# Four half weight tiles ahead of the second half of the prompt, and turned parameter rows, at the start of a one-core decoder step

## The chip, the cores and the metric

The kernel runs on one core of a Trainium2 chip. A core has TensorE (PE: matrix products and transposes), VectorE (DVE), ScalarE (ACT), GpSimd (POOL) and SyncE (SP); SP and POOL issue most of the transfers between main memory and the core's memory. The metric is the device time of one execution in microseconds; the result is a median over executions.

## The reference, cut to what matters

One layer of a decoder trunk. The prompt (512 tokens) and eight samples are normalised, multiplied by one wide input matrix, and fed to three branches. All of it is in float32. The edit touches only the first steps: the normalisation, and the first product with the columns for q and k.

```python
def rmsnorm(x, g):
    xf = x.astype(jnp.float32)
    y = xf * lax.rsqrt(jnp.mean(xf * xf, axis=-1, keepdims=True) + EPS)
    return (y * g.astype(jnp.float32)).astype(x.dtype)
...
    h = rmsnorm(x, g_norm[l])
    a_u, a_v, a_z, b_q, b_k, b_v, b_gd, b_z, c_q, c_z, gl = split_proj(h, w_in[l])
...
    mk, mv = mem_kv(mem, g_mem[l], w_mem_kv[l])
```

`split_proj` is `h @ w_in` cut into pieces; D_MODEL is 1024. The memory tokens (256) are normalised with g_mem and multiplied with w_mem_kv.

## The kernel before, in words

The large products go through 17 blocks (NAMES: QK, K, V, BV, ...) of eight weight tiles. A weight tile is 1024 rows by 128 columns, held as eight 128x128 pieces. Each float32 product is made from three products of a high and a low part: ScalarE copies raw weights into w_hi (function `hi`, L512), VectorE subtracts to get w_lo (`lo`, L1156), and TensorE multiplies w_hi by h_lo, w_lo by h_hi and w_hi by h_hi. A tile takes 24 products over the first 256 tokens and 24 over the other 256 with the eight samples (264 columns). SP loads raw weights two tiles at a time into two buffers: tiles 0 and 1 from the first load, 2 and 3 from the second. Tile t is split two tiles ahead of its product; semaphore split_done counts the splits, prod_done the tiles done, evac_done those copied out of PSUM.

Every engine runs its own list in program order, and semaphores tie them together. There is no scheduler: the order in the code is the order on the engine.

The start is written by hand. The samples come first: ScalarE squares them (`square`, L517), VectorE scales them (L1490), TensorE turns them in eight transposes (L1084). Then for the first 256 tokens: ScalarE squares one block of 128 rows and VectorE the other (L1475), ScalarE takes the root (L536), VectorE the reciprocal (L1478), VectorE scales one block of rows (L1480) and ScalarE the other (L539), TensorE turns 16 pieces (L1094), ScalarE writes the high part with the gain g_norm (`x_hi_part`, L545) and VectorE the low part (`x_lo_part`, L1485). The transposes go through four banks of PSUM, so that each from the fifth on waits for a low part. TensorE then multiplies tiles 0 and 1 over these 256 tokens (L1101), turns the second 256 and multiplies the same two tiles over them; tiles 2 to 7 go as whole tiles through `project` (L865). Behind tile 3 stand the first transposes of the memory tokens (L888), whose squares ScalarE makes after it has copied out tile 1.

The gains are read by POOL as columns, one number to a partition: gn1, gm1, bg1, gnc, each with a transfer of its own:

```python
pool.dma_start(gn1[:, :], g_norm[0].rearrange("(k p) -> p k", p=P)).then_inc(sem("gn_loaded"), 16)
```

Of the kernel before, what the change touches and what calls it, by code (L numbers as in the profile page):

```python
# [68 lines left out]
X_A, X_B, X_M = 1, 1 + KT, 1 + 2 * KT  # L69
# [29 lines left out]
def bass_gated_parallel_step(nc, x_prompt, x_sample, state_gla, cache_mem_k, cache_mem_v,  # L99
# [19 lines left out]
    with ExitStack() as ctx:  # L119
# [47 lines left out]
        gn1 = sb("gn1", [P, KT])  # L167
        gm1 = sb("gm1", [P, KT])
        bg1 = sb("bg1", [P, 3 * KT])
        gnc = sb("gnc", [P, 2])  # L170
# [97 lines left out]

        def x_bank(u):

            return (p45, p67)[u // 2 % 2][:, u % 2, 0:HX]
# [50 lines left out]
        def _(pool):  # L322
# [22 lines left out]
            with nc.allow_non_contiguous_dma(reason="parameters by channel, a few KB"):  # L345
                pool.dma_start(gm1[:, :], g_mem[0].rearrange("(k p) -> p k", p=P)).then_inc(sem("gm_loaded"), 16)
                pool.dma_start(bg1[:, :], b_gate[0].rearrange("(k p) -> p k", p=P)).then_inc(sem("params_loaded"), 16)
                pool.dma_start(gnc[:, :], gn_g[0].rearrange("(k p) -> p k", p=P)).then_inc(sem("params_loaded"), 16)
                pool.dma_start(w00[:, :], w_s[0, :, 0, 0:1].rearrange("h o -> o h").broadcast_to([P, AH])).then_inc(sem("params_loaded"), 16)
                pool.dma_start(gd_raw[:, :, :], win[:, O_GD:O_GD + P].rearrange("(k p) c -> p k c", p=P)).then_inc(sem("params_loaded"), 16)  # L350
# [144 lines left out]
        def _(act):  # L495
# [24 lines left out]
            def mem_squares():  # L520
                act.wait_ge(sem("mem_loaded"), 16)
                link(square(mem_in[:, 0, :], junk, 5))
                act.wait_ge(sem("mem_sq"), 1)
                A(rstd[:, 5:5 + MT], ssq[:, 5:5 + MT], ACT.Sqrt, scale=1.0 / D, bias=eps_col[:, :]).then_inc(sem("rt_mem"), 1)

            def mem_hi_part(k):
                act.wait_ge(sem("gm_loaded"), 16)
# [3 lines left out]
            def x_roots(a):  # L531
# [6 lines left out]
                act.wait_ge(sem("x_rs"), a + 1)  # L538
                A(x0_in[:, 2 * a + 1, :], x0_in[:, 2 * a + 1, :], ACT.Copy,  # L539
                  scale=rstd[:, 2 * a + 1:2 * a + 2]).then_inc(sem("x_n_act"), 1)  # L540

            def x_hi_part(u):
                k, c0 = (u - X_A) % KT, HX * ((u - X_A) // KT)
                act.wait_ge(sem("xT_done"), u + 1)
                A(h_hi[:, k, c0:c0 + HX], x_bank(u), ACT.Copy, scale=gn1[:, k:k + 1]).then_inc(sem("xT_hi"), 1)  # L545

            act.wait_ge(sem("eps_ready"), 1)
            link(A(lstd, eps_col, ACT.Sqrt))
            act.wait_ge(sem("xs_loaded"), 16)
# [6 lines left out]
            for k in range(KT):  # L556
                x_hi_part(X_A + k)
                if k == 3:
                    hi(0, 0, 16)
# [1012 lines left out]
```

## Time and profile before

| what | value |
|---|---|
| median of 3 runs | 909.87 us (909.71 to 911.19) |
| the profiled execution's own time | 909.98 us |
| its span, first to last instruction | 908.2 us |
| PE busy | 870.3 us, 96% |
| DVE busy | 417.9 us, 46% |
| ACT busy | 395.7 us, 44% |
| POOL busy | 95.9 us, 11% |
| mean granted TensorE clock | 0.990 |

The busy time of an engine is the time in which it works at an instruction; waits and the issue of transfers are not in it. The two microseconds between the span and the execution's time lie around the program. The times in the trace count from the start of the span.

### The profile page before, as it was taken

How to read it: one execution, taken by the hardware profiler on the slowest of the kernel's cores; microseconds unless marked ns; L12 is line 12 of the kernel's file. 1: busy time of each engine (PE TensorE's matmuls, PEld its weight loads, DVE VectorE, ACT ScalarE, POOL GpSimd, SP SyncE). 2: the span in 40 equal slices, each digit the busy share in tenths (PEclk: the TensorE clock that was granted, in tenths of full speed). 3: DMA queues.
4: the chain of work that ended last, by engine and by line, in shares of the span. 5: the costliest groups of instructions: out<-in, count | busy, mean ns of one | idle time of the engine just before them, and what ended most of it. 6: DMA issues, size and time to landing. Idle time of an engine off the chain costs nothing.

```text
span 908.2 us, 16712 instructions
## 1 busy us (share of the span) xinstructions
PE 870.3 (96%) x7062; PEld 842.0 (93%) x7062; DVE 417.9 (46%) x711; ACT 395.7 (44%) x674; POOL 95.9 (11%) x136
## 2 busy tenths in 40 slices
PE   4999999999999999999999999999999999999991
PEld 3999999999999999999999999999899999999990
DVE  5434324324244346633326878554444454455333
ACT  5535332227656766242232266332234473433334
POOL 3001000000000101300001247001120000000000
PEclk9999999999999999999999999999999999999995
DMA  9425652231232434952446861516561432352102
GB/s 263 130 58 173 193 186 93 62 126 47 65 122 84 152 116 139 383 172 95 162 146 221 325 213 47 179 57 232 185 232 58 129 111 76 109 185 86 64 2 94
DMA packets 86164, 126.57 MB, mean 139 GB/s; under 512 B 3216, under 2 KB 72848, under 8 KB 86096
## 3 DMA queue, kind: packets, MB, share of 16 engines
q1 hardware_dynamic: 71824, 75.50, 26.3%
q0 software_dynamic: 13984, 49.02, 15.2%
q8 instruction: 53, 0.87, 0.4%
q10 hardware_dynamic: 288, 1.05, 0.3%
q14 instruction: 15, 0.12, 0.0%
HBM read 113.37 MB, written 12.19 MB: 138 GB/s over the span
## 4 chain that ended last, share of the span: by engine, by line
PE 93%; ACT 2%; DMA 2%; DVE 1%; issue 1%; DVEq 0%; POOL 0%; ACTq 0%; POOLq 0%
PE mm L865 79%; PE mm L1101 1%; PE p L876 1%; DMA out_dram<-tok 1%; PE p L841 1%; PE p L843 1%; PE p L842 1%; PE p L1019 1%; PE p L1049 1%; PE p L993 1%; PE p L990 1%; PE p L966 1%; PE p L1114 1%; DMA stok<-in_x_sample_dram 1%; PE p L989 1%
## 5 line engine op out<-in xcount | busy, mean ns | idle before, releaser
L865 PE MATMUL mm<-h_lo,w_hi 128*128 128x260 f32 (+1 forms) x1504 | 309.5, 287 | 0.5 <-DVE w_lo L1156 0.5
L865 PE MATMUL mm<-h_hi,w_hi 128*128 128x260 f32 (+1 forms) x1504 | 302.7, 283 | 0.0
L865 PE MATMUL mm<-h_hi,w_lo 128*128 128x260 f32 (+1 forms) x1504 | 302.0, 282 | 0.0
L865 PEld LDWEIGHTS mm<-h_lo,w_hi 128*128 128x128 f32 x1504 | 232.1, 188 | 10.3 <-issue 8.0
L865 PEld LDWEIGHTS mm<-h_hi,w_lo 128*128 128x128 f32 x1504 | 231.7, 188 | 0.0
L865 PEld LDWEIGHTS mm<-h_hi,w_hi 128*128 128x128 f32 x1504 | 231.5, 188 | 0.0
L1156 DVE TENSOR_TENSOR w_lo<-raw,w_hi 128x1024 fp32r<-128x1024 f32 x136 | 165.7, 1219 | 83.9 <-ACT w_hi L512 69.9
L512 ACT ACTIVATE w_hi<-raw 128x1024 fp32r<-128x1024 f32 x136 | 143.6, 1056 | 19.3 <-DMA raw<-in_w_in_dram 11.7
L865 PE MATMUL mm<-x_lo,w_hi 128*128 128x260 f32 (+1 forms) x512 | 114.6, 285 | 0.0
L865 PE MATMUL mm<-x_hi,w_hi 128*128 128x260 f32 (+1 forms) x512 | 113.3, 282 | 0.0
L865 PE MATMUL mm<-x_hi,w_lo 128*128 128x260 f32 (+1 forms) x512 | 113.1, 282 | 0.0
L592 ACT ACTIVATE stage<-mm 128x520 f32<-128x520 f32 x40 | 24.2, 606 | 157.4 <-PE mm L865 157.4
L865 PEld LDWEIGHTS mm<-x_lo,w_hi 128*128 128x128 f32 x512 | 83.2, 188 | 2.6 <-issue 2.6
L865 PEld LDWEIGHTS mm<-x_hi,w_hi 128*128 128x128 f32 x512 | 83.3, 188 | 0.0
L865 PEld LDWEIGHTS mm<-x_hi,w_lo 128*128 128x128 f32 x512 | 83.2, 188 | 0.0
L607 ACT ACTIVATE gate<-mm,bg 128x520 f32<-128x520 f32 x24 | 16.7, 695 | 44.0 <-PE mm L865 43.7
L602 ACT ACTIVATE t<-mm 128x520 f32<-128x520 f32 x16 | 9.7, 605 | 50.7 <-PE mm L865 50.5
L1186 DVE TENSOR_TENSOR gate<-gate,stage 128x520 f32<-128x520 f32 (+1 forms) x16 | 11.2, 700 | 42.9 <-ACT stage L592 42.9
L1173 DVE COPY stok<-p 8x128 f32 (+1 forms) x16 | 4.4, 277 | 49.0 <-PE p L878 49.0
L604 ACT ACTIVATE stage<-mm 128x520 f32<-128x520 f32 x16 | 9.7, 606 | 39.5 <-PE mm L865 39.4
L876 PE MATMUL p<-ident,stage 128*128 128x128 f32 x128 | 21.0, 276 | 2.2 <-ACT stage L590 1.0
L1430 DVE CUSTOM_DVE_ANT_0 gate<-gate,work 128x256 f32<-128x256 f32 x64 | 22.7, 408 | 0.0
(299 smaller groups left out, 879.2 us busy)
## 6 DMA issues: line engine op xcount, KB each, us to landing
raw<-in_w_in_dram SPq DMA_DIRECT2D x44, 1024.0 KB, 5.3
raw<-in_w_branch_dram SPq DMA_DIRECT2D x12, 1024.0 KB, 5.1
raw<-in_w_mem_kv_dram SPq DMA_DIRECT2D x8, 1024.0 KB, 5.8
gate<-in_cache_mem_k_dram POOLq DMA_DIRECT2D x16, 512.0 KB, 6.4
tok<-in_cache_mem_v_dram POOLq DMA_DIRECT2D x14, 512.0 KB, 5.3
tok<-in_state_gla_dram POOLq DMA_DIRECT2D x8, 512.0 KB, 6.9
out_dram<-tok POOLq DMA_DIRECT2D x8, 512.0 KB, 6.9
work<-scr_q POOLq DMA_DIRECT2D x8, 512.0 KB, 5.2
```

The lines of the kernel that those rows point to most:

```text
L512: A(w_hi[:, j], raw[:, j // 2, :, (j % 2) * P:(j % 2 + 1) * P], ACT.Copy).then_inc(hi_ready, 1)
L592: ins = A(st, src, ACT.Copy)
L602: ins = A(out3(t1), src, ACT.Silu)
L604: ins = A(st, src, ACT.Gelu_apprx_tanh)
L607: ins = A(out3(gate), src, ACT.Sigmoid, bias=bg1[:, i * KT + c:i * KT + c + 1])
L841: MM(out, w[0], x[1], start=first_mm, stop=False)
L842: MM(out, w[1], x[0], start=False, stop=False)
L865: ins = MM(mm[:, j % 2, a, 0:c1 - c0], wp[:, j, k, :], xp[:, k, c0:c1], start=(k == 0 and wp is w_hi and xp is xl), stop=(k == KT - 1 and ...
L876: ins = TRP(p45[:, j % 2, n * P:(n + 1) * P], stage[:, j % 2, n * P:(n + 1) * P], ident[:, :])
L1156: V.tensor_tensor(w_lo[:, j], raw[:, j // 2, :, (j % 2) * P:(j % 2 + 1) * P], f32(w_hi[:, j]), ALU.subtract).then_inc(split_done, 1)
L1186: V.tensor_tensor(g2, g2, s, ALU.mult).then_inc(stage_used, 1)
L1430: V.tensor_tensor_reduce(k, k, q_bc[:, b % 3, h * CD:(h + 1) * CD], 1.0, 0.0, ALU.mult, ALU.add, sc[:, m, b * CH + h:b * CH + h + 1]).then ...
```

## The change

Five things change, all before the ninth product tile.

1. Parameters. g_norm, g_mem, b_gate and gn_g are read as 42 rows of 128 numbers into `prm_rows` (a piece of the stage buffer), TensorE turns them in one transpose, ScalarE copies the result into `prm`, of which gn1, gm1, bg1 and gnc are now views. The four transfers and the one for the samples are issued first on POOL and share one semaphore, start_loaded (80).
2. Order on ScalarE and VectorE. The samples' square comes after the splits of tiles 0 to 2 on ScalarE; the samples' scaling and that of the third block of 128 prompt rows go to POOL.
3. Scaling of the first two blocks is cut into halves of 512 columns: three on VectorE, one on ScalarE. The first four transposes wait for the first two halves.
4. Four weight tiles (X_T = 4) instead of two are multiplied over the first 256 tokens. Tiles 0 and 2, and 1 and 3, share a bank pair: their first halves stand in the two banks and are copied out early (`evac_first`), before the second halves use those banks. The samples are turned between tile 1 and tile 2, the second 256 tokens after tile 3.
5. The 128 columns of w_in for the gate (gd_raw) and w00 are issued on POOL after its two scalings.

The core of the diff (names and waits that only follow from it are left out):

```diff
-X_A, X_B, X_M = 1, 1 + KT, 1 + 2 * KT
+X_A, X_S, X_B, X_M = 0, KT, KT + 1, 2 * KT + 1
+X_T = 4
...
-                pool.dma_start(stok[:, :], x_sample.rearrange("b t d -> (b t) d")).then_inc(sem("xs_loaded"), 16)
-                pool.dma_start(gn1[:, :], g_norm[0].rearrange("(k p) -> p k", p=P)).then_inc(sem("gn_loaded"), 16)
+                for at, src in ((0, g_norm), (KT, g_mem), (2 * KT, b_gate), (5 * KT, gn_g)):
+                    rows = src[0].rearrange("(k p) -> k p", p=P)
+                    pool.dma_start(prm_rows[at:at + rows.shape[0], :], rows).then_inc(sem("start_loaded"), 16)
+                pool.dma_start(stok[:, :], x_sample.rearrange("b t d -> (b t) d")).then_inc(sem("start_loaded"), 16)
...
+            pool.wait_ge(sem("x_rs"), 2)
+            pool.tensor_scalar(stok[:, :], stok[:, :], rstd[0:B, NT:NT + 1], None, ALU.mult).then_inc(sem("xs_n"), 1)
+            pool.wait_ge(sem("x_rs"), 3)
+            pool.tensor_scalar(x0_in[:, 2, :], x0_in[:, 2, :], rstd[:, 2:3], None, ALU.mult).then_inc(sem("x_n"), 1)
...
+            act.wait_ge(sem("prm_T"), 1)
+            A(prm[:, :], prm_bank, ACT.Copy).then_inc(sem("prm_ready"), 1)
+            act.wait_ge(sem("prm_ready"), 1)
+            x_roots(0)
+            act.wait_ge(sem("x_rs"), 1)
+            A(x0_in[:, 1, 512:D], x0_in[:, 1, 512:D], ACT.Copy, scale=rstd[:, 1:2]).then_inc(sem("x_n_act"), 1)
+            hi(0, 0, 16)
+            for k in range(KT):
+                x_hi_part(X_A + k)
+            hi(1, 1, 16)
+            hi(2, 2, 16)
+            act.wait_ge(sem("start_loaded"), 80)
+            link(square(stok[:, :], junk[0:B, :], NT))
+            A(rstd[0:B, NT:NT + 1], ssq[0:B, NT:NT + 1], ACT.Sqrt, scale=1.0 / D, bias=eps_col[0:B, :]).then_inc(sem("rt_x"), 1)
+            hi(3, 3, 16)
+            x_roots(1)
+            evac_first(0)
             act.wait_ge(sem("xsT_full"), 1)
             A(h_hi[:, :, T:TT], hs[:, :, :], ACT.Copy).then_inc(sem("xT_hi"), 1)
+            evac_first(1)
             for k in range(KT):
                 x_hi_part(X_B + k)
+                if k == 3:
+                    evac_first(2)
+            evac_first(3)
...
+            def first_half(j, a):
+
+                c0, c1, u0 = (0, HX, X_A) if a == 0 else (HX, TT, X_B)
+                pe.wait_ge(split_done, j + 1)
+                if a == 1:
+                    pe.wait_ge(sem("first_evac"), j + 1)
+                for k in range(KT):
+                    if j == 0:
+                        pe.wait_ge(sem("xT_lo"), u0 + k + 1)
+                    for wp, xp in ((w_hi, h_lo), (w_lo, h_hi), (w_hi, h_hi)):
+                        ins = MM(mm[:, j % 2, j // 2, 0:c1 - c0], wp[:, j, k, :], xp[:, k, c0:c1],
+                                 start=(k == 0 and xp is h_lo), stop=(k == KT - 1 and wp is w_hi and xp is h_hi))
+                ins.then_inc(prod_done if a == 1 else sem("first_done"), 1)
+
+            pe.wait_ge(sem("ident_ready"), 1)
+            pe.wait_ge(sem("start_loaded"), 80)
+            TRP(prm_bank, prm_rows, ident[0:42, 0:42]).then_inc(sem("prm_T"), 1)
+            pe.wait_ge(sem("x_n"), 2)
             for k in range(KT):
+                if k == 4:
+                    pe.wait_ge(sem("x_n_act"), 1)
+                    pe.wait_ge(sem("x_n"), 3)
+                x_turn(X_A + k)
+            for j in range(X_T):
+                first_half(j, 0)
+                if j == 1:
+                    pe.wait_ge(sem("xs_n"), 1)
+                    pe.wait_ge(sem("xT_lo"), X_S - 3)
+                    for k in range(KT):
+                        ins = TRP(x_bank(X_S)[:, k * B:(k + 1) * B], stok[:, k * P:(k + 1) * P], ident[0:B, 0:B])
                     ins.then_inc(sem("xT_done"), 1)
+            pe.wait_ge(sem("x_n"), 5)
+            for k in range(KT):
+                x_turn(X_B + k)
+            for j in range(X_T):
+                first_half(j, 1)
...
+            x_square(0)
+            x_root(0)
+            x_scale(0, 0, 512)
+            x_scale(1, 0, 512)
+            x_scale(0, 512, D)
+            dve.wait_ge(sem("prm_ready"), 1)
+            lo(0, 0)
+            for k in range(KT):
+                x_lo_part(X_A + k)
+            lo(1, 1)
+            dve.wait_ge(sem("rt_x"), 2)
+            V.reciprocal(rstd[0:B, NT:NT + 1], rstd[0:B, NT:NT + 1]).then_inc(sem("x_rs"), 1)
+            lo(2, 2)
+            x_square(1)
+            lo(3, 3)
+            x_root(1)
+            x_scale(3, 0, D)
```

The instructions on ScalarE, from its first on, in the kernel before. The semaphores on which an instruction waits stand in brackets; stok are the samples, mz the prompt rows.

```order
L548 ACTIVATE small<-small 128x1 [waits eps_ready]
L517 ACTIVATE tok,small<-stok 8x1024 [waits xs_loaded,act_link]
L551 ACTIVATE small<-small 8x1 [waits act_link]
L517 ACTIVATE tok,small<-mz 128x1024 [waits x_loaded0]
L536 ACTIVATE small<-small 128x2 [waits x_sq,act_link]
L539 ACTIVATE mz<-mz,small 128x1024 [waits x_rs]
L554 ACTIVATE h_hi<-hs 128x8x8 [waits xsT_full]
L545 ACTIVATE h_hi<-p,gn 128x256 [waits xT_done,gn_loaded]
L545 ACTIVATE h_hi<-p,gn 128x256 [waits xT_done] x3
L512 ACTIVATE w_hi<-raw 128x1024 [waits w_loaded0]
L545 ACTIVATE h_hi<-p,gn 128x256 [waits xT_done] x4
```

The same place in the changed kernel:

```order
L553 ACTIVATE small<-small 128x1 [waits eps_ready]
L555 ACTIVATE prm<-p 128x42 [waits prm_T,act_link]
L522 ACTIVATE tok,small<-mz 128x1024 [waits x_loaded0,prm_ready]
L540 ACTIVATE small<-small 128x2 [waits x_sq,act_link]
L559 ACTIVATE mz<-mz,small 128x512 [waits x_rs]
L517 ACTIVATE w_hi<-raw 128x1024 [waits w_loaded0]
L546 ACTIVATE h_hi<-p,prm 128x256 [waits xT_done] x8
L517 ACTIVATE w_hi<-raw 128x1024 [waits w_loaded0]
L517 ACTIVATE w_hi<-raw 128x1024 [waits w_loaded1]
L522 ACTIVATE tok,small<-stok 8x1024 [waits start_loaded]
L567 ACTIVATE small<-small 8x1 [waits act_link]
L517 ACTIVATE w_hi<-raw 128x1024 [waits w_loaded1]
```

The samples' square and root have moved behind the first 256 tokens and three weight splits, and the copy of the parameters now stands ahead of the prompt's square.

POOL's list at its start, the kernel before (from its first transfer):

```order
L334 DMA stok<-in_x_sample_dram 8x1024
L335 DMA gn<-in_g_norm_dram 128x8x1
L337 MEMSET ident 128x128
L337 MEMSET tri 128x256
...
L346 DMA gm<-in_g_mem_dram 128x8x1
L347 DMA bg<-in_b_gate_dram 128x24x1
L348 DMA gnc<-in_gn_g_dram 128x2x1
L349 DMA w<-in_w_s_dram 128x8x1
L350 DMA gd_raw<-in_w_in_dram 128x8x128
```

And in the changed kernel:

```order
L338 DMA stage<-in_g_norm_dram 8x128
L338 DMA stage<-in_g_mem_dram 8x128
L338 DMA stage<-in_b_gate_dram 24x128
L338 DMA stage<-in_gn_g_dram 2x128
L339 DMA stok<-in_x_sample_dram 8x1024
...
L350 TENSOR_SCALAR stok<-stok,small 8x1024 [waits x_rs]
L352 TENSOR_SCALAR mz<-mz,small 128x1024 [waits x_rs]
L354 DMA gd_raw<-in_w_in_dram 128x8x128
L355 DMA w<-in_w_s_dram 128x8x1
```

The samples' transfer has gone from the first place to the fifth, the column-wise loads have become rows, and two scalings stand ahead of the two loads that remain.

## Rows read from the trace of the kernel before

**Rows 1.** The page, the chain that ended last, by engine.
```profile
PE 93%; ACT 2%; DMA 2%; DVE 1%; issue 1%; DVEq 0%; POOL 0%; ACTq 0%; POOLq 0%
```
**Rows 2.** Timeline to 18 us: start, duration, engine, line, operation, idle before.
```profile
1.33 0.65 POOL L334 DMA_DIRECT2D stok<-in_x_sample_dram  x1 [0.81 <-POOLq L1560]
2.44 1.15 SPq L300 DMA_DIRECT2D raw<-in_w_in_dram  x1
...
3.61 0.30 POOL L338 TENSOR_SCALAR_AFFINE_SELECT ident<-ident 128x128 f32<-128x128 f32 x1 [0.23 <-POOL tri L337]
...
4.56 0.93 POOL L346 DMA_DIRECT2D gm<-in_g_mem_dram  x1
...
7.10 1.05 ACT L517 ACTIVATE tok<-stok 8x1024 f32<-8x1024 f32 x1 [4.78 <-DMA stok<-in_x_sample_dram]
...
8.28 0.29 ACT L551 ACTIVATE small<-small 8x1 f32<-8x1 f32 x1
8.48 1.04 ACT L517 ACTIVATE tok<-mz 128x1024 f32<-128x1024 f32 x1
...
10.02 0.99 PE L1084 MATMUL p<-ident,stok 8*128 8x8 f32 x8 [10.02 <-DVE stok L1490]
...
11.11 0.30 ACT L536 ACTIVATE small<-small 128x2 f32<-128x2 f32 x1 [1.49 <-DVE small L1475]
...
11.64 0.75 DVE L1480 TENSOR_SCALAR mz<-mz,small 128x1024 f32<-128x1024 f32 x1
11.64 1.15 ACT L539 ACTIVATE mz<-mz,small 128x1024 f32<-128x1024 f32 x1 [0.23 <-DVE small L1478]
...
15.28 1.05 ACT L512 ACTIVATE w_hi<-raw 128x1024 fp32r<-128x1024 f32 x1
...
16.36 1.23 DVE L1156 TENSOR_TENSOR w_lo<-raw,w_hi 128x1024 fp32r<-128x1024 f32 x1 [0.46 <-ACT w_hi L512]
...
17.64 0.39 PE L1101 MATMUL mm<-h_lo,w_hi 128*128 128x256 f32 x1 [1.21 <-DVE w_lo L1156]
```
**Rows 3.** The same timeline, from 23 to 44 us.
```profile
23.31 0.28 PE L1101 MATMUL mm<-h_hi,w_hi 128*128 128x256 f32 x1
...
24.36 3.23 DVE L1485 SCALAR_TENSOR_TENSOR h_lo<-p,gn,h_hi 128x256 fp32r<-128x256 f32 x8 [1.55 <-ACT h_hi L545]
...
26.27 0.37 PE L1101 MATMUL mm<-h_lo,w_hi 128*128 128x264 f32 x1
...
28.01 1.23 DVE L1156 TENSOR_TENSOR w_lo<-raw,w_hi 128x1024 fp32r<-128x1024 f32 x1 [0.42 <-ACT w_hi L512]
...
32.17 0.40 PE L865 MATMUL mm<-h_lo,w_hi 128*128 128x256 f32 x2
...
43.70 0.60 PE L888 MATMUL p<-ident,gate 128*128 128x128 f32 x4
```
**Rows 4.** Transfers issued before 60 us: issuer, count, size, us to landing.
```profile
stok<-in_x_sample_dram POOLq DMA_DIRECT2D x1, 32.0 KB, 5.7
...
gm<-in_g_mem_dram POOLq DMA_DIRECT2D x1, 4.0 KB, 7.2
```
**Rows 5.** Timeline, 535 to 539 us: POOL and VectorE side by side.
```profile
535.20 3.27 POOL L438 TENSOR_TENSOR tok<-tok,work 128x1024 f32<-128x1024 f32 x1 [5.50 <-DVE tok L1402]
...
536.90 2.12 DVE L1180 TENSOR_TENSOR t<-t,stage 128x520 f32<-128x520 f32 x1 [0.69 <-ACT stage L604]
...
538.55 2.73 POOL L439 TENSOR_TENSOR tok<-tok,work 128x1024 f32<-128x1024 f32 x1
```
**Rows 6.** The page's costliest groups: busy and mean ns of one, idle before.
```profile
L1186 DVE TENSOR_TENSOR gate<-gate,stage 128x520 f32<-128x520 f32 (+1 forms) x16 | 11.2, 700 | 42.9 <-ACT stage L592 42.9
```
**Rows 7.** The raw weight tile to 30 us: time of its three loads to landing.
```profile
DMA to landing us min/median/max: 5.9/8.7/18.3
```
**Rows 8.** Windows of 1 us: busy per engine, granted clock, DMA share, GB/s.
```profile
3.00:4.00 1.00, 0.00 (x0) 0.00 (x0) 0.00 (x0) 0.00 (x0) 0.77 (x4) 1.00 1.06 422
...
12.00:13.00 1.00, 0.07 (x1) 0.10 (x2) 0.52 (x2) 0.93 (x2) 0.00 (x0) 1.00 1.11 105
```

More of the change, by code:

```diff
@@ L344, in _ @@
             pool.memset(tri[0:SUB, 0, SUB:P], 0.0).then_inc(sem("tri_ready"), 1)
[L345 to L348, printed above, removed]
+            pool.wait_ge(sem("x_rs"), 2)
+            pool.tensor_scalar(stok[:, :], stok[:, :], rstd[0:B, NT:NT + 1], None, ALU.mult).then_inc(sem("xs_n"), 1)
+            pool.wait_ge(sem("x_rs"), 3)
+            pool.tensor_scalar(x0_in[:, 2, :], x0_in[:, 2, :], rstd[:, 2:3], None, ALU.mult).then_inc(sem("x_n"), 1)
+            with nc.allow_non_contiguous_dma(reason="a row's first column and sixteen columns of a weight"):
+                pool.dma_start(gd_raw[:, :, :], win[:, O_GD:O_GD + P].rearrange("(k p) c -> p k c", p=P)).then_inc(sem("params_loaded"), 16)
                 pool.dma_start(w00[:, :], w_s[0, :, 0, 0:1].rearrange("h o -> o h").broadcast_to([P, AH])).then_inc(sem("params_loaded"), 16)
-                pool.dma_start(gd_raw[:, :, :], win[:, O_GD:O_GD + P].rearrange("(k p) c -> p k c", p=P)).then_inc(sem("params_loaded"), 16)
             pool.wait_ge(sem("memT_done"), KT)
@@ L1081, in _ @@
             pe.wait_ge(sem("ident_ready"), 1)
-            pe.wait_ge(sem("xs_n"), 1)
-            for k in range(KT):
-                ins = TRP(x_bank(0)[:, k * B:(k + 1) * B], stok[:, k * P:(k + 1) * P], ident[0:B, 0:B])
-            ins.then_inc(sem("xT_done"), 1)
-            for a, u0 in enumerate((X_A, X_B)):
-                c0, c1 = (0, HX) if a == 0 else (HX, TT)
-                pe.wait_ge(sem("x_n"), a + 1)
-                pe.wait_ge(sem("x_n_act"), a + 1)
-                for k in range(KT):
-                    wait(pe, sem("xT_lo"), u0 + k - 3)
-                    for n in range(2):
-                        ins = TRP(x_bank(u0 + k)[:, n * P:(n + 1) * P], x0_in[:, 2 * a + n, k * P:(k + 1) * P], ident[:, :])
-                    ins.then_inc(sem("xT_done"), 1)
-                for j in range(2):
-                    pe.wait_ge(split_done, j + 1)
-                    for k in range(KT):
-                        pe.wait_ge(sem("xT_lo"), u0 + k + 1)
-                        for wp, xp in ((w_hi, h_lo), (w_lo, h_hi), (w_hi, h_hi)):
-                            ins = MM(mm[:, j, a, 0:c1 - c0], wp[:, j, k, :], xp[:, k, c0:c1],
-                                     start=(k == 0 and xp is h_lo), stop=(k == KT - 1 and wp is w_hi and xp is h_hi))
-                    if a == 1:
-                        ins.then_inc(prod_done, 1)
@@ new lines, in x_turn @@
+            def x_turn(u):
+                a, k = (0, u - X_A) if u < X_S else (1, u - X_B)
+                wait(pe, sem("xT_lo"), u - 3)
+                for n in range(2):
+                    ins = TRP(x_bank(u)[:, n * P:(n + 1) * P], x0_in[:, 2 * a + n, k * P:(k + 1) * P], ident[:, :])
+                ins.then_inc(sem("xT_done"), 1)
+            def first_half(j, a):
[10 more added lines that the diff above has]
+                ins.then_inc(prod_done if a == 1 else sem("first_done"), 1)
@@ L1468, in _, with x_square @@
             V.memset(gdT, 1.0).then_inc(sem("gd_ones"), 1)
-            def x_scale(a):
+            def x_square(a):
                 dve.wait_ge(sem(f"x_loaded{a}"), 16)
```

85 lines of the change are left out of this document (34 added, 51 removed).

## The prediction

> **What bounds the kernel now.** I read the chain that ended last first: TensorE holds 93% of it [rows 1]. Then the timeline of the start, where the edit is [rows 2, 3]. TensorE issues its first weight product at 17.64 us and from 23.31 us on runs almost without a gap: transposes of the second 256 tokens, products from 26.27, two whole weight tiles from 32.17, and at 43.70 the first transposes of the memory tokens, which also stand behind tile 3 in the changed kernel. What follows 43.70 is the same program in both. So the question is one number: when does TensorE reach the transposes that now begin at 43.70? A delay or a gain there passes to the end one for one, since TensorE bounds the rest.
>
> Up to 17.64 TensorE waits for a chain [rows 2]. The samples land, ScalarE squares them at 7.10, squares the prompt rows at 8.48, takes the root at 11.11; both engines scale from 11.64, ScalarE's 1024 columns needing 1.15 us. Then transposes, h_hi, h_lo, and last the weight split: w_hi at 15.28, w_lo 16.36 to 17.59, product at 17.64. From 17.64 to 43.70 are 26.06 us.
>
> **The change, part by part.** Call S the moment at which ScalarE starts to square the first prompt rows (8.48 now).
>
> *S itself.* ScalarE now waits for the transposed parameters (prm_T) before that square, and prm_T waits for five POOL transfers under one semaphore, the samples last. Nothing else hides this wait: ScalarE has no earlier work. One issue of eight rows costs 0.65 us [rows 2], so the fifth begins at 1.33 + 4 x 0.65 = 3.93. The samples took 5.7 us from issue to landing when they went first, the memory gains, issued at 4.56, took 7.2 [rows 4]; those are 1,024 pieces of 4 bytes, the new ones only rows. Landing is thus at 9.6 to 11.1; I take 9.8, near the lower end because the transfer is the same eight rows. TensorE's transpose, the copy of 128x42 and the hand-overs I estimate at 0.7 (a small transpose and a small ScalarE operation of 0.2 to 0.3 each, as the 8.28 root of 0.29). S = 10.5, two microseconds later than now. The bounds are S = 8.0, if all five land at 7.1 as the first does now, and 11.8.
>
> A page of the Trainium skill would have it sooner: "DMA: Bandwidth & Descriptors", "Anatomy of one DMA", gives a SWDGE transfer a fixed cost of about 2.0 us. The trace disagrees under the load at the start: 5.7 and 7.2 [rows 4].
>
> *From S to the first product* [rows 2]. Square to root takes 7.10 to 8.28, 1.18. Root to scaling takes 11.11 to 11.64, 0.53. ScalarE's half-width scaling, between half of 1.15 and 1.15, I take as 0.65; VectorE's three halves, each 0.38 to 0.75, are 1.35 at most 1.5, and end before the split needs VectorE. w_hi starts at S + 2.36, w_lo 1.08 behind it (15.28 to 16.36) at S + 3.44, done S + 4.67. Only now come the h_lo parts, and TensorE's transposes 4 to 7 each wait for one. In the second round of the kernel before, first h_lo at 24.36 to first product at 26.27, this took 1.91 [rows 3]. First product: S + 6.55 = 17.05. So 0.6 earlier than 17.64: the samples and half of the scaling are out of the way, the two weight splits on the path are one, but S has moved by 2.0.
>
> *Behind the first product.* [rows 2, 3] The products before the whole tiles end, and the 16 transposes, are the same work in another order; 26.06 us of TensorE stay. Added to it:
> The eight sample transposes, which now lie before 17.64 in waiting time, come into the stream: 0.99 [rows 2], I take 0.95.
> Tile 1 needs its split. After the second round, w_lo ended at 28.01 + 1.23, 2.97 behind the first product; a half tile takes 5.67/47 x 24 = 2.9 (17.64 to 23.31, 48 products). Stall 0.12.
> The sample transposes wait for POOL. ScalarE, counted from the first product: hi(1,1) at +0.66 (1.08 ahead of 28.01), hi(2,2) 1.05 later, then the samples' square at +2.75, root at +3.93, POOL may start at +4.6 (0.53 and a hand-over of 0.15), that is S + 11.15. TensorE is there at S + 12.5. POOL's scaling of 8x1024 is the cost that no row shows. Below stands the 0.30 of a one-input POOL operation on 128 columns, above the 2.73 of a two-input one on 128x1024 [rows 2, 5]. Eight times 0.30, 2.4, counts the start eight times; with a third of it start I get 1.6. Beside it VectorE starts lo(2,2), 1.23, just before. The row at 535.20 took 3.27 against 2.73 for its like when a w_lo ran at its start: 0.55 more [rows 5]. Ready at S + 13.3, started at 13.4: stall 0.9, with bounds 0 and 2.1.
> The first evacuations add four ScalarE copies and take four away; they stand in ScalarE's free time between products.
>
> Sum: 43.70 is replaced by 10.5 + 6.55 + 26.06 + 0.95 + 0.12 + 0.9 = 45.1, which is 1.4 later.
>
> The port is told by the Trainium skill, "SBUF — State Buffer", "Who interferes with whom": a VectorE instruction with two SBUF inputs and a GpSimd one that reads SBUF exclude each other, the first to start wins. The trace agrees: the VectorE product at 536.90 needed 2.12 while POOL worked, 0.70 elsewhere [rows 5, 6]. Without the rule the sum is 0.55 less, +0.85.
>
> *What costs nothing, and what hides it.* With POOL in the way x_square(1) and lo(3,3) slip to about S + 14.5 and 15.7; tile 3 wants its split at S + 17.2. POOL then scales the third 128 prompt rows, behind VectorE's own scaling, from about S + 16.7 to 18.3 (or 19.4, at 2.73); TensorE wants them at S + 20.1. Cover 0.7 to 1.8; at 3.4 for that row nothing would be left. The second weight pair landed at 2.44 + 18.3 = 20.7 [rows 2, 7], while hi(2,2) now asks at S + 8.3 = 18.8 instead of 26.9. Between 12 and 13 us the queues moved 105 GB/s where 3 to 4 us had 422 [rows 8]; that is the stretch in which the 4-byte pieces and the gate-down block trickled through. They are gone or later, so I expect landing near 16.5, hidden. The memory tokens' squares follow the evacuation of tile 1's second half; from there to lo(4) are some 0.4 for the copy, 1.18 and 0.53 as above, two scalings of 0.75 and a w_lo of 1.23, together 4.8 us, against 5.9 of products (26.27 to 32.17): hidden by 1.1. The gate-down load is issued behind POOL's second scaling, near 29, and is wanted only in block K, far behind 43.70.
>
> The profiled execution took 909.98 with a span of 908.2, 0.1 above the median 909.87. Forecast: 909.98 + 1.4 = 911.4. I call a difference of 0.2%, 1.8 us, the least that a measurement of this kernel can tell.
>
> **The rivals.**
> *The small loads come one per turn.* The three earliest POOL loads were not served together; the third landed at 4.56 + 7.2 = 11.8, although it was issued only 3.2 us after the first [rows 2, 4]. If each of the five takes a turn behind the large transfers, the samples land at 11.8 or later: S = 12.5, +3.4, 913.4; slower. For it: five transfers queue where two did. Against: they carry 42 short rows, not thousands of pieces. It decides from a landing of 10.2 on. The same page of the skill ("Queues, rings and completion order") says that an engine takes turns between its queues by packets.
> *POOL's scaling is slow.* 2.73 plus the lock: the sample transposes start 1.1 later, +2.5, 912.5; slower. For it: every POOL elementwise row here takes 2.7 or more. Against: one input, not two. It decides from 2.0 us on.
> *The second weight pair still lands at 20.7.* hi(2,2), the samples' square and POOL all slip by 1.9: +3.3, 913.3. Against: the queue has less before it.
> *The loads land early.* If all five land with the first, near 7.1, S is 7.8 to 8.0, and w_hi waits for its weights no more than now; then -1.1 to -1.3, 908.8. With POOL's stall gone too, -2.1, 907.9, faster. For it: little data. Against: the 7.2 of the third transfer.
> *Nothing moves*, because gain and added stream cancel, is inside the forecast.
>
> **How the numbers follow.** The forecast, a shift between -1.8 and +1.8 with +1.4 the likeliest, gets 0.45; early loads alone count in it. Late loads 0.16, slow POOL 0.16, late weights 0.07: slower together 0.39 (each alone would pass 1.8, the forecast's sum being only 0.4 below it). Early loads with no POOL stall, or a chain that I have overpriced by over three microseconds, 0.16. So faster 0.16, same 0.45, slower 0.39. The range takes in early loads without the second mishap at its lower end and late loads at its upper: 908.2 to 913.9; the forecast's own is 909.9 to 912.3.
>
> **What would show it.** The prompt's first square starts near 10.5 on ScalarE, after a wait ended by TensorE's transpose; earlier means early loads. The first weight product starts near 17.05. Two half tiles run back to back with at most 0.2 between; before the sample transposes a wait of 0.9 that a POOL instruction on stok ends. The memory transposes start near 45.1. VectorE's CUSTOM or w_lo row beside POOL's first scaling is longer than 1.23. I am wrong if ScalarE's square starts before 9, if POOL scales stok in under 1 us or over 2.5, or if w_hi of tile 2 waits for a DMA.

## The result, and the profile after

The changed kernel takes 917.72 us (median of 4 runs, 917.02 to 918.36), the kernel before 909.98 us in the same comparison: 1.0082 times as long, interval 1.0065 to 1.01. That is 7.7 us slower, where 1.4 was forecast, and outside the range of 908.2 to 913.9. The profiled execution took 917.02 us with a span of 915.3.

The timeline of the changed kernel up to its first product, which answers to [rows 2]:

```profile
3.51 0.52 POOL L339 DMA_DIRECT2D stok<-in_x_sample_dram  x1
...
9.51 0.30 PE L1123 MATMUL p<-ident,stage 42*128 42x42 f32 x1 [9.51 <-DMA stok<-in_x_sample_dram]
9.90 0.21 ACT L555 ACTIVATE prm<-p 128x42 f32<-128x42 f32 x1 [7.59 <-PE p L1123]
10.14 1.06 ACT L522 ACTIVATE tok<-mz 128x1024 f32<-128x1024 f32 x1
...
13.63 1.23 DVE L1194 TENSOR_TENSOR w_lo<-raw,w_hi 128x1024 fp32r<-128x1024 f32 x1 [0.50 <-ACT w_hi L517]
...
16.99 0.56 PE L1117 MATMUL mm<-h_lo,w_hi 128*128 128x256 f32 x1
17.34 0.41 PE L1117 MATMUL mm<-h_hi,w_lo 128*128 128x256 f32 x1
17.56 0.41 PE L1117 MATMUL mm<-h_hi,w_hi 128*128 128x256 f32 x1
...
19.53 0.28 PE L1117 MATMUL mm<-h_lo,w_hi 128*128 128x256 f32 x1
19.65 0.28 PE L1117 MATMUL mm<-h_hi,w_lo 128*128 128x256 f32 x1
```

ScalarE's square of the prompt starts at 10.14 and the first product at 16.99. Look then at the distance between the products: 0.22 us from 17.34 to 17.56, but 0.12 from 19.53 to 19.65. The first eleven products run at about half the rate of those that follow.

The same timeline around the wait for the samples, VectorE, POOL and TensorE together, to the memory transposes (they answer to [rows 3]):

```profile
21.13 0.15 DVE L1541 RECIPROCAL small<-small 8x1 f32<-8x1 f32 x1 [1.08 <-ACT small L567]
21.21 1.20 DVE L1194 TENSOR_TENSOR w_lo<-raw,w_hi 128x1024 fp32r<-128x1024 f32 x1
...
21.38 6.01 POOL L350 TENSOR_SCALAR stok<-stok,small 8x1024 f32<-8x1024 f32 x1 [15.66 <-DVE small L1541]
...
22.33 1.20 DVE L1513 CUSTOM_DVE_ANT_0 tok<-mz 128x1024 f32<-128x1024 f32 x1
...
23.48 1.21 DVE L1194 TENSOR_TENSOR w_lo<-raw,w_hi 128x1024 fp32r<-128x1024 f32 x1
...
24.79 1.72 DVE L1522 TENSOR_SCALAR mz<-mz,small 128x1024 f32<-128x1024 f32 x1
27.39 2.83 POOL L352 TENSOR_SCALAR mz<-mz,small 128x1024 f32<-128x1024 f32 x1
27.45 1.02 PE L1136 MATMUL p<-ident,stok 8*128 8x8 f32 x8 [3.50 <-POOL stok L350]
28.40 0.58 PE L1117 MATMUL mm<-h_lo,w_hi 128*128 128x256 f32 x1
...
50.73 0.60 PE L905 MATMUL p<-ident,gate 128*128 128x128 f32 x4
```

POOL needs 6.01 us for 8x1024 numbers, and TensorE stands still for 3.50 us until it is done. The memory transposes start at 50.73, 7.03 later than in [rows 3], and the profiled execution is 7.04 longer: the whole loss lies ahead of them.

Windows of the changed kernel in that stretch, columns as in [rows 8]:

```profile
25.00:26.00 1.00, 0.00 (x0) 0.00 (x0) 1.00 (x1) 0.00 (x0) 1.00 (x1) 1.00 0.27 34
26.00:27.00 1.00, 0.00 (x0) 0.00 (x0) 0.51 (x1) 0.00 (x0) 1.00 (x1) 0.57 0.81 203
27.00:28.00 1.00, 0.55 (x5) 0.56 (x6) 0.00 (x0) 0.00 (x0) 1.00 (x2) 0.50 1.08 381
28.00:32.00 4.00, 4.00 (x22) 3.98 (x22) 0.45 (x2) 0.53 (x2) 4.00 (x3) 0.50 0.39 118
32.00:33.00 1.00, 1.00 (x6) 1.00 (x6) 0.00 (x0) 0.00 (x0) 0.07 (x1) 0.52 0.79 168
33.00:34.00 1.00, 1.00 (x11) 1.00 (x10) 0.00 (x0) 0.00 (x0) 0.00 (x0) 1.00 1.34 333
```

TensorE has been idle since 23.95. Within its wait, between 26 and 27 us, the granted clock falls to 0.50 (the 1.2 GHz level), and it stays there until about 33 us, through the sample transposes and 21 products. The windows count TensorE's instructions: 22 in the four microseconds from 28 to 32, 11 in the one microsecond from 33 on, at full clock.

The chain that ended last says the same from the other side. It now has a piece on POOL, and the 48 products behind it (tiles 2 and 3) take 7.91 us. In the kernel before, 48 products had 5.67 us from the first start to the last [rows 2, 3]; the same 48 as here take 5.87 in the chain of experiment 1, where the clock holds:

```profile
21.38 6.02 POOL stok L350
27.40 0.04 issue
27.45 1.02 PE p L1136 x8
28.47 7.91 PE mm L1117 x48
```

### The profile page after: what moved, and what is told of

Its sections match the earlier page's. It is cut to its first block, busy times and chain, and to the rows that moved or that the text cites. A ratio compares the mean times of both kernels' runs of the same rounds, so it can differ in the third digit from the quotient of the medians.

```text
span 915.3 us, 16709 instructions
## 1 busy us (share of the span) xinstructions
PE 873.8 (95%) x7063; PEld 845.6 (92%) x7063; DVE 418.2 (46%) x712; ACT 394.4 (43%) x674; POOL 102.9 (11%) x138
## 3 DMA queue, kind: packets, MB, share of 16 engines
q10 hardware_dynamic: 288, 1.05, 0.3%
## 4 chain that ended last, share of the span: by engine, by line
PE 92%; ACT 2%; DMA 2%; POOL 1%; DVE 1%; issue 1%; DVEq 0%; ACTq 0%; POOLq 0%
PE mm L882 77%; PE mm L1117 2%; PE p L893 1%; DMA out_dram<-tok 1%; PE p L858 1%; PE p L860 1%; PE p L859 1%; PE p L1036 1%; PE p L1066 1%; PE p L1007 1%; PE p L1010 1%; PE p L983 1%; POOL stok L350 1%; DMA stok<-in_x_sample_dram 1%; PE p L1152 1%
## 5 line engine op out<-in xcount | busy, mean ns | idle before, releaser
L882 PE MATMUL mm<-h_lo,w_hi 128*128 128x260 f32 (+1 forms) x1472 | 303.0, 287 | 0.5 <-DVE w_lo L1194 0.5
L882 PE MATMUL mm<-h_hi,w_hi 128*128 128x260 f32 (+1 forms) x1472 | 296.3, 283 | 0.0
L882 PE MATMUL mm<-h_hi,w_lo 128*128 128x260 f32 (+1 forms) x1472 | 295.5, 282 | 0.0
L882 PEld LDWEIGHTS mm<-h_lo,w_hi 128*128 128x128 f32 x1472 | 227.2, 188 | 10.3 <-issue 8.0
L882 PEld LDWEIGHTS mm<-h_hi,w_lo 128*128 128x128 f32 x1472 | 226.6, 188 | 0.0
L882 PEld LDWEIGHTS mm<-h_hi,w_hi 128*128 128x128 f32 x1472 | 226.6, 188 | 0.0
L623 ACT ACTIVATE gate<-mm,prm 128x520 f32<-128x520 f32 x24 | 16.7, 694 | 44.0 <-PE mm L882 43.7
```

What stands on the lines that cost most here:

```text
L623: ins = A(out3(gate), src, ACT.Sigmoid, bias=bg1[:, i * KT + c:i * KT + c + 1])
L882: ins = MM(mm[:, j % 2, a, 0:c1 - c0], wp[:, j, k, :], xp[:, k, c0:c1], start=(k == 0 and wp is w_hi and xp is xl), stop=(k == KT - 1 and ...
```

## The experiments

The kernels were timed in two groups, 1 to 4 and 5 to 8, with the kernel before among them; its median was 910.46 us (22 runs) in the first and 911.2 in the second. So kernels are compared within a group, by their ratio to the kernel before, or by the start of the memory transposes in their traces. The two don't always agree: executions of the kernel before alone lie between 908.9 and 912.2 us in the first group, and behind the memory transposes the traces differ by up to two microseconds (the table at the end of this section). For a step at the start the start of the memory transposes is the surer measure.

**1. Samples scaled on VectorE.** POOL's first scaling goes to VectorE, right behind the reciprocal.

```diff
-            pool.wait_ge(sem("x_rs"), 2)
-            pool.tensor_scalar(stok[:, :], stok[:, :], rstd[0:B, NT:NT + 1], None, ALU.mult).then_inc(sem("xs_n"), 1)
...
             V.reciprocal(rstd[0:B, NT:NT + 1], rstd[0:B, NT:NT + 1]).then_inc(sem("x_rs"), 1)
+            dve.wait_ge(sem("x_rs"), 2)
+            V.tensor_scalar(stok[:, :], stok[:, :], rstd[0:B, NT:NT + 1], None, ALU.mult).then_inc(sem("xs_n"), 1)
             lo(2, 2)
```

> The changed kernel, with the samples' scaling on VectorE, right behind their reciprocal and before lo(2,2), instead of on POOL. Theory A: the 3.5 us wait for POOL's 6.01 us instruction and the half clock behind it (21 products at 0.214 instead of 0.118 us, 2.0 us) are the main loss; both go, and the time is 917.7 - 5.5 = 912.2; the granted clock stays at full speed from 26 to 33 us, and the products behind the samples' transposes run at 0.118. Rival: the order with four half tiles itself costs the time (early copies, transposes inside the stream), then it stays above 916.

Measured: 911.40 us, ratio 1.001 (0.9999 to 1.002). The timeline:

```profile
21.15 0.74 DVE L1541 TENSOR_SCALAR stok<-stok,small 8x1024 f32<-8x1024 f32 x1
...
23.78 0.66 PE L1134 MATMUL p<-ident,stok 8*128 8x8 f32 x8
...
44.67 0.60 PE L903 MATMUL p<-ident,gate 128*128 128x128 f32 x4
```

VectorE's scaling takes 0.74, TensorE doesn't wait, its clock stays up, the eight sample transposes take 0.66 in place of 1.02, and the memory transposes start at 44.67, 6.06 earlier than in the changed kernel. The first eleven products still run slowly. One instruction on POOL was thus worth about six of the seven microseconds; what that six is made of, the next two ask.

**2. VectorE waits for POOL.** The scaling stays on POOL; VectorE has nothing to do while it runs.

```diff
             V.reciprocal(rstd[0:B, NT:NT + 1], rstd[0:B, NT:NT + 1]).then_inc(sem("x_rs"), 1)
+            dve.wait_ge(sem("xs_n"), 1)
             lo(2, 2)
```

> The changed kernel, but VectorE waits for POOL's scaling of the samples (xs_n) before lo(2,2), so that POOL works alone. Theory A (VectorE's two-input instructions keep POOL from its memory port): POOL's row on the samples falls from 6.01 to about 2.8 us, as its full 128x1024 row took; the transposes of the samples start near 24.3 instead of 27.45, the clock is not lost, and the time is about 912.6, lo(2,2) being a little late now. Rival: the instruction takes 6 us by itself on 8 partitions; then it ends at 27.4 as before, tile 2's split comes 1.2 us behind it, and the time is 918 to 919.

Measured: 913.07 us, ratio 1.0034 (1.0021 to 1.0046). The timeline:

```profile
21.16 2.85 POOL L350 TENSOR_SCALAR stok<-stok,small 8x1024 f32<-8x1024 f32 x1 [15.44 <-DVE small L1541]
24.11 0.66 PE L1136 MATMUL p<-ident,stok 8*128 8x8 f32 x8
...
25.33 0.39 PE L1117 MATMUL mm<-h_lo,w_hi 128*128 128x256 f32 x1 [0.56 <-DVE w_lo L1194]
...
45.78 0.60 PE L905 MATMUL p<-ident,gate 128*128 128x128 f32 x4
```

So the operation costs 2.85 by itself, and 3.16 of its 6.01 come from VectorE's instructions beside it. TensorE doesn't wait for the samples, its clock doesn't fall, and the memory transposes start 4.95 earlier than in the changed kernel. They are still 1.11 later than in experiment 1: holding VectorE back costs TensorE a wait of 0.56 for tile 2's split, and fifteen products ran slowly at the start in this trace, not eleven. So this run shows the price of contention and not that of a free repair.

**3. The wait filled.** The changed kernel, with 28 products into an unused bank ahead of TensorE's wait for the samples.

```diff
                 if j == 1:
+                    for _ in range(28):
+                        MM(p67[:, 0, HX:2 * HX], w_hi[:, 1, 0, :], h_hi[:, 0, 0:HX], start=True, stop=True)
                     pe.wait_ge(sem("xs_n"), 1)
```

> The changed kernel with 28 extra products into an unused half bank (their result is read by nobody) between tile 1 and the samples' transposes, where TensorE waits 3.5 us for POOL. POOL's instruction stays as it is. Theory A: the wait stays, but TensorE has work in it, keeps 2.4 GHz, and the following 21 products take 0.118 instead of 0.214: 917.7 - 2.0 = 915.7. Rival: the slow products come from something else that the wait brings (memory traffic, the waits for splits): no change, 917.7.

Measured: 915.35 us, ratio 1.0045 (1.0028 to 1.0061). The timeline, with the wait still ended by the same POOL instruction of 6.01 us:

```profile
23.93 3.52 PE L1134 MATMUL p<-h_hi,w_hi 128*128 128x256 f32 x28
27.64 0.66 PE L1138 MATMUL p<-ident,stok 8*128 8x8 f32 x8 [0.20 <-POOL stok L350]
...
48.53 0.60 PE L905 MATMUL p<-ident,gate 128*128 128x128 f32 x4
```

The eight sample transposes take 0.66 in place of 1.02, and the memory transposes come 2.20 earlier, with POOL's instruction as long as before. Counted from the end of that instruction they come after 20.95 in place of 23.34 us, 2.4 less: 2.0 in the products and 0.36 in the sample transposes. The fall of the clock is thus a cost of its own, about 2.3 us of a kernel that lost 7.0.

**4. A warm start.** Experiment 1, and transposes of the identity into an unused bank in TensorE's idle time: 18 ahead of its first wait, 11 behind the turned parameters.

```diff
+            for _ in range(18):
+                TRP(p67[:, 0, HX:HX + P], ident[:, :], ident[:, :])
             pe.wait_ge(sem("start_loaded"), 80)
             TRP(prm_bank, prm_rows, ident[0:42, 0:42]).then_inc(sem("prm_T"), 1)
+            for _ in range(11):
+                TRP(p67[:, 0, HX:HX + P], ident[:, :], ident[:, :])
```

> As the kernel with the samples' scaling on VectorE, and with 18 extra transposes of the identity before the parameters' transpose and 11 behind it, into an unused half bank, in TensorE's idle time from 5 to 12.8 us. Theory A: the first 11 products run at 1.2 GHz (0.214 us apart) only because TensorE had done little before; with the extra transposes they run at 0.118 and the time is 1.0 us under that of the kernel without them, about 911.2. Rival: the first products are paced by the h_lo parts and not by the clock: no change, 912.2.

Measured: 909.68 us, ratio 0.9993 (0.9982 to 1.0004), 1.7 less than experiment 1 in the same group. The first product starts at 16.59, the products are 0.12 apart from the second on, and the memory transposes start at 43.53, 1.14 earlier than in experiment 1. One microsecond had been expected. The medians give more than the trace, and the trace is the surer measure of this step.

**5. The prompt's square first.** Experiment 1, and ScalarE does what needs only the prompt and the weights ahead of its wait for the parameters; TensorE turns the parameter rows between the prompt's fourth and fifth piece, no longer first.

```diff
-            act.wait_ge(sem("prm_T"), 1)
-            A(prm[:, :], prm_bank, ACT.Copy).then_inc(sem("prm_ready"), 1)
-            act.wait_ge(sem("prm_ready"), 1)
             x_roots(0)
             act.wait_ge(sem("x_rs"), 1)
             A(x0_in[:, 1, 512:D], x0_in[:, 1, 512:D], ACT.Copy, scale=rstd[:, 1:2]).then_inc(sem("x_n_act"), 1)
             hi(0, 0, 16)
+            act.wait_ge(sem("prm_T"), 1)
+            A(prm[:, :], prm_bank, ACT.Copy).then_inc(sem("prm_ready"), 1)
+            act.wait_ge(sem("prm_ready"), 1)
...
                 if k == 4:
+                    pe.wait_ge(sem("start_loaded"), 80)
+                    TRP(prm_bank, prm_rows, ident[0:42, 0:42]).then_inc(sem("prm_T"), 1)
                     pe.wait_ge(sem("x_n_act"), 1)
...
```

> The samples' scaling on VectorE as in the first experiment, and ScalarE takes the prompt's square, root, half scaling and the first weight tile's high part ahead of its wait for the turned parameter rows; TensorE turns those rows after four of the eight pieces of the prompt. Theory A (the wait for the parameters, which are ready at about 9.95 us, holds back work that needs only the prompt's first block, there at 5.96, and every us won ahead of the first product is won at the end): the split of the transposed pieces starts at about 9.95 in place of 13.34, the first product at 13.4 in place of 16.82, and the time falls by 3.4, to about 908.0. Rival B (the second pair of weight tiles, landed at about 15.1, or the third block's scaling on GpSimd at 25.5 is late next): 910.0 or more, with a new wait of TensorE at 16 to 22 us or ahead of the second half's transposes.

Measured: 909.15 us, ratio 0.9977 (0.9967 to 0.9987). The timeline of its start:

```profile
8.72 1.94 PE L1102 MATMUL p<-ident,mz 128*128 128x128 f32 x8 [8.72 <-DVE mz L1520]
9.41 1.06 ACT L515 ACTIVATE w_hi<-raw 128x1024 fp32r<-128x1024 f32 x1 [1.00 <-DMA raw<-in_w_in_dram]
10.59 0.33 PE L1124 MATMUL p<-ident,stage 42*128 42x42 f32 x1
10.95 0.21 ACT L557 ACTIVATE prm<-p 128x42 f32<-128x42 f32 x1 [0.48 <-PE p L1124]
...
14.55 0.56 PE L1115 MATMUL mm<-h_lo,w_hi 128*128 128x256 f32 x1
```

The first product stands at 14.55, 2.27 earlier than in experiment 1 and not 3.4: the turned parameters now stand behind eight cold transposes on TensorE, so ScalarE has them at 10.95 and not at 9.95. And the memory transposes, at 43.28, gain only 1.39, since twenty products run at half rate in place of eleven: nine more of them, by 0.214 less 0.118, are 0.87. The expectation missed the first product by 1.15 us and the gain at the memory transposes by 2.0. That the wait for the parameters holds the start back is right; that every microsecond won ahead of the first product is won at the end is not, since 0.88 of it went into products at half rate. The ratios say more than the trace, 3.0 us less than experiment 1: behind the memory transposes the two traces differ by 1.9 us, which nothing here explains.

**6. The same with a warm start.** Experiment 5, with 14 transposes of the identity ahead of TensorE's first wait and 6 behind the turned parameters.

```diff
             pe.wait_ge(sem("ident_ready"), 1)
+            for _ in range(14):
+                TRP(mm[:, 1, 1, 0:P], ident[:, :], ident[:, :])
             pe.wait_ge(sem("x_n"), 2)
...
                     TRP(prm_bank, prm_rows, ident[0:42, 0:42]).then_inc(sem("prm_T"), 1)
+                    for _ in range(6):
+                        TRP(mm[:, 1, 1, 0:P], ident[:, :], ident[:, :])
```

> The experiment before (square first) with 14 transposes of the identity ahead of the prompt's transposes and 6 behind the turned parameters, into a bank that the products overwrite later. Theory A (the first eleven products run at 0.214 us because TensorE did little before them): the first products run at 0.118, and the time is about 1.0 below that of the kernel with the square first, so about 907. Rival B (the head start is used up by a wait of TensorE for a split or for a scaling): no difference between the two, within 0.3.

Measured: 906.62 us, ratio 0.9953 (0.9938 to 0.9967), the shortest time of all, 2.5 below experiment 5. The timeline:

```profile
5.16 3.22 PE L1121 MATMUL mm<-ident 128*128 128x128 f32 x14 [5.16 <-POOL ident L342]
...
8.87 1.45 PE L1102 MATMUL p<-ident,mz 128*128 128x128 f32 x8 [0.48 <-DVE mz L1524]
...
13.87 0.36 PE L1115 MATMUL mm<-h_lo,w_hi 128*128 128x256 f32 x1
14.07 0.28 PE L1115 MATMUL mm<-h_hi,w_lo 128*128 128x256 f32 x1
14.19 0.29 PE L1115 MATMUL mm<-h_hi,w_hi 128*128 128x256 f32 x1
```

The prompt's first transposes take 1.45 in place of 1.94, the first product comes 0.68 earlier, and the products of the first tile are 0.12 apart from the second on. With 20 slow products fewer, 1.9 us by the same difference, that is 2.6; the memory transposes start at 40.83, 2.45 earlier. One microsecond had been expected, because the slow products had been counted as eleven and not as twenty.

**7. Two half tiles.** Experiment 1 with X_T = 2, the splits left as they are: what the two more half tiles are worth.

```diff
-X_T = 4
+X_T, X_SP = 2, 4
...
-                if k == 3:
-                    evac_first(2)
-            evac_first(3)
...
-                        if name != "QK" or g + j + 2 >= X_T:
+                        if name != "QK" or g + j + 2 >= X_SP:
```

> The samples' scaling on VectorE as in the first experiment, but only two weight tiles stand over the prompt's first 256 tokens, as in the kernel before, in place of four; the splits of all four tiles stay where they are. Theory A (the two more half tiles cover the scaling, GpSimd's 2.8 to 3.4 us for the third block above all, which ends at about 28.9): TensorE waits about 4.4 us ahead of the second half's transposes, its clock falls after it as it did after the wait for the samples (2.0 us), and the time is about 917.8. Rival B (the cover isn't needed): 911.4, as the first experiment.

Measured: 916.35 us, ratio 1.0055 (1.0039 to 1.007). The timeline:

```profile
25.46 3.40 POOL L350 TENSOR_SCALAR mz<-mz,small 128x1024 f32<-128x1024 f32 x1 [19.73 <-DVE small L1513]
...
28.91 3.74 PE L1099 MATMUL p<-ident,mz 128*128 128x128 f32 x16 [4.07 <-POOL mz L350]
```

TensorE waits 4.07 us for POOL's third block, its clock shows 0.51 from 30 to 34 us, and the memory transposes come at 50.47, 5.80 later than in experiment 1. A wait of 4.4 and 917.8 us had been expected. The two half tiles do cover what they have to cover; their own price is nothing that these traces show.

**8. Parameters by element.** Experiment 5, with the parameter vectors loaded in 4-byte pieces into their columns, in the same order, and nothing turned.

```diff
-                    rows = src[0].rearrange("(k p) -> k p", p=P)
-                    pool.dma_start(prm_rows[at:at + rows.shape[0], :], rows).then_inc(sem("start_loaded"), 16)
+                    cols = src[0].rearrange("(k p) -> p k", p=P)
+                    pool.dma_start(prm[:, at:at + cols.shape[1]], cols).then_inc(sem("start_loaded"), 16)
...
-            act.wait_ge(sem("prm_T"), 1)
-            A(prm[:, :], prm_bank, ACT.Copy).then_inc(sem("prm_ready"), 1)
-            act.wait_ge(sem("prm_ready"), 1)
+            act.wait_ge(sem("start_loaded"), 80)
...
```

> The kernel with the square first, but the parameter vectors are loaded element by element into their columns, as before the change, all five small loads in the same order at the start; nothing is turned, and ScalarE and VectorE wait for the loads in place of the turned rows. Theory A (pieces of 4 bytes are what the small loads cost): the last small load lands at about 13, not 9.3, the loads of the prompt and the weights are slowed beside it, the first product stands near 16.5, and the time is 911 to 912.5, about 3 to 4 above the kernel with the square first. Rival B (the form of the load doesn't matter): within 0.5 of the kernel with the square first.

Measured: 912.17 us, ratio 1.0011 (1.0 to 1.0021), 3.0 more than experiment 5. Timeline and window, columns as in [rows 8]:

```profile
5.42 0.55 POOL L339 DMA_DIRECT2D stok<-in_x_sample_dram  x1
...
12.39 1.06 ACT L515 ACTIVATE w_hi<-raw 128x1024 fp32r<-128x1024 f32 x1 [3.74 <-DMA raw<-in_w_in_dram]
14.03 1.22 DVE L1188 TENSOR_TENSOR w_lo<-raw,w_hi 128x1024 fp32r<-128x1024 f32 x1 [4.80 <-DMA stok<-in_x_sample_dram]
...
17.38 0.56 PE L1113 MATMUL mm<-h_lo,w_hi 128*128 128x256 f32 x1
```

```profile
8.00:9.00 1.00, 0.02 (x1) 0.05 (x1) 1.00 (x3) 0.65 (x1) 0.14 (x1) 1.00 1.02 68
```

The samples, last of the five, land 8.6 us after an issue that is itself 1.91 later, at 14.0 where about 13 had been expected; in the window of 8 to 9 us the queues move 68 GB/s, and even the first weight tile comes three microseconds later (12.39 against 9.41). The first product starts at 17.38, 2.83 later than in experiment 5 (16.5 had been expected), and the memory transposes at 45.38, 2.10 later, since thirteen products ran slowly and not twenty. So reading the vectors as rows is worth 2 to 3 us, with the transpose and the copy that it needs paid. It is worth that where nothing waits needlessly for the rows: in experiment 1, where ScalarE's first work does wait for them, the memory transposes stand 0.97 behind the kernel before.

**The traces side by side.** Slow products are those from the first weight product on until one follows the last after 0.12 us (a single longer first gap is left aside); the rest is the span behind the start of the memory transposes.

| kernel | first product | slow products | memory transposes | rest |
|---|---|---|---|---|
| before | 17.64 | none | 43.70 | 864.5 |
| changed | 16.99 | 11 | 50.73 | 864.6 |
| 1, samples on VectorE | 16.82 | 11 | 44.67 | 865.7 |
| 2, VectorE waits | 16.77 | 15 | 45.78 | 864.7 |
| 3, wait filled | 17.17 | 10 | 48.53 | 865.4 |
| 4, warm start | 16.59 | none | 43.53 | 863.8 |
| 5, square first | 14.55 | 20 | 43.28 | 863.8 |
| 6, the same, warm | 13.87 | none | 40.83 | 864.0 |
| 7, two half tiles | 16.79 | 16 | 50.47 | 864.3 |
| 8, by element | 17.38 | 13 | 45.38 | 865.6 |

The changed kernel and experiments 1, 2 and 7 are alike up to the first product, and yet 11 to 16 of their products are slow. The number is no property of the kernel alone; half a microsecond between two traces can come from it.

## Why the prediction was wrong

**Right: the start.** Landing near 9.8, S near 10.5, first product at 17.05; measured 9.37 in the chain, 10.14 and 16.99. The weights of tile 2 landed in time, so the rivals of late loads, late weights and early loads all fell. The copy, the halves and the split cost what the rows of before had said. That the first product came within 0.06 is in part luck: the forecast's S was 0.36 too late, because an issue took 0.52 and not 0.65, and the stretch from S on 0.30 too short (6.85, not 6.55), for the most part because the last eight transposes took 1.94; in the round of before that had served as the model, at full rate, they took 1.61.

**The step that failed: "Ready at S + 13.3, started at 13.4: stall 0.9, with bounds 0 and 2.1".** It has three errors, and TensorE waited 3.50.

First, the operation. A time between 0.30 and 2.73 was taken as 1.6, with eight starts of a 128-column operation as the model; experiment 2 shows 2.85, and 128x1024 takes 2.83 in the trace above. Eight rows cost POOL as much as 128, and one input as much as two. The text had said against the slow rival "one input, not two", a reason without a row.

Second, the contention. It was priced as one overlap, 0.55, from a row in which POOL met one w_lo [rows 5]. Here POOL's instruction met VectorE's four in a row. Its 6.01 end 2.7 us behind the end of lo(3,3) (24.69 to 27.39), about its time alone. That reads as if it did next to nothing until VectorE's three two-input instructions were through; a row shows only start and end, so this is an inference. That VectorE's instructions together cost it 3.16 is shown (experiment 2). VectorE's own scaling, the fourth, took 1.72 in place of 0.75. The list of what VectorE does next stood in the prediction itself, as work that POOL would make late, "x_square(1) and lo(3,3) slip to about S + 14.5 and 15.7"; it was the other way round: the three rows took 1.20, 1.20 and 1.21, and the prediction's sign, a row longer than 1.23, did not come. The Trainium skill, "SBUF — State Buffer", "Who interferes with whom", says that whoever issues first has the shared ports for the whole instruction. The trace agrees that the first one, lo(2,2), wasn't slowed and the second one, POOL's, was. The delay over three successors of the first is what the trace adds to it. VectorE's scaling fits less well: it ended 0.88 before POOL's instruction, so it wasn't shut out for the whole of it.

Third, the sum of the rival. It took 2.73 and the one overlap and came to 912.5; the mechanism was the right one, the size was not.

**The term that was missing: the clock.** No step priced what TensorE's clock does. From the wait of 3.50 on the granted clock stood at 0.50 until about 33 us: 21 products 0.214 apart in place of 0.118 are 2.0 us. Experiment 3 wins them back by keeping TensorE at work through the same wait. The sample transposes too ran at that level, 1.02 us against 0.66 in experiments 1 and 3; their term of 0.95 came out right by luck, its source being a row of before (0.99) that was just as slow.

At the start eleven products ran at that distance as well, 1.05 us. In the changed kernel these slow products made nothing later. The chain that leads to POOL's instruction goes from the prompt's transposes over ScalarE's copies, splits, square and root and VectorE's reciprocal, and holds no product; at full rate TensorE would only have waited longer by as much. It costs where that wait is gone: experiment 4 wins back 1.14 of experiment 1, and experiment 6 wins 2.45 of experiment 5, with transposes ahead. In the kernel before no product was slow: its prompt transposes ran at half rate, 0.213 us from start to start, until 16.0 us, the last two 0.11 apart, and its products from 17.64 on were 0.12 apart (48 in 5.67 us [rows 2, 3]). Its samples' transposes stood ahead of these; the change moved them away. Whether that is why the changed kernel reaches full rate later, at 19.4 us, no run tests by itself.

**The books.** Forecast for the memory transposes 45.1, measured 50.73, a difference of 5.6. POOL's instruction ends at 27.39 where S + 13.3, 23.8, had been put: it starts 0.3 earlier and takes 6.01 in place of 1.6 + 0.55, which makes the sample transposes 3.55 late. From their start on, 23.28 us where the sum had 21.2: 2.1 more, the clock. Together 5.65. (The wait itself was only 2.6 longer than its term, 3.50 and not 0.9, because TensorE too came to it late, by the slow products of the start.) The other terms (first product, 26.06 of stream) hold within 0.1. Tile 1's stall of 0.12, for which its own numbers give 0.07, did not come. "What follows 43.70 is the same program in both" holds for these two traces, 7.03 against 7.04. In the eight experiments the rest is between 863.8 and 865.7 us long; these two microseconds aren't explained by anything here.

**What the change would be worth.** Rows for the vectors, four half tiles and halved scaling are in experiment 6, together with the samples' scaling on VectorE, the square ahead of the wait and the warm transposes: 0.9953 of the kernel before. Together they are faster than before: 4.6 us by the medians of the group, 2.9 by the start of the memory transposes. For experiment 5 the two say 2.1 and 0.4. Which of them the gain needs, beyond the pairs compared above, wasn't tried. Nor was the third block's scaling on another engine.

## What to carry to other kernels

Before work is given to an idle engine, look up that engine's own rows for its price whatever the number of rows, and list all that the engine with which it shares ports does until the work is done: the wait may be paid once for each of these instructions. Where TensorE's stream gets a new wait, look in the trace at the rate of the products behind it, and look at that of the first products too: here they ran at half rate. If they are slow and nothing else bounds the stretch, try products or transposes into an unused bank in the idle time; here that won back 1.1 to 2.5 us. A gain at the start counts only where no later wait takes it up. Put no wait for parameters ahead of work that doesn't need them.

## What the hardware showed that was not expected

- GpSimd's scaling of one input takes 2.83 us for 128x1024 and 2.85 for 8x1024 (experiment 2), against 0.74 to 0.75 on VectorE for the same shapes.
- Beside four VectorE instructions it takes 6.01. Beside one VectorE scaling that starts 0.07 earlier it takes 3.41 in place of 2.83 (experiments 1 and 5), and that scaling keeps its 0.75. The VectorE instructions beside the 6.01 were three of 1.2 us that keep their length and one scaling, which takes 1.72 in place of 0.75.
- At the start of the changed kernel the granted clock reads 1.00 in every window, and yet the products are 0.214 us apart until 19.4 us, 256 columns at the 1.2 GHz level. Only the distance of the products shows it. In the other kernels without added transposes at the start (experiments 1, 2, 3, 5, 7 and 8) full rate begins between 19.0 and 20.3 us, although their first products stand between 14.55 and 17.38: an earlier first product, as in experiment 5, in part only bought more slow products. With 20 to 29 added transposes in TensorE's idle time (experiments 6 and 4) none was slow.
- Five small loads (four of rows, and the samples) land 5.0 to 5.9 us after their issue in the changed kernel. With the four parameter vectors in pieces of 4 bytes the same five take 7.1 to 8.6 (experiment 8).
